# Two decoder layers on one core: first tiles in pieces, whole inverse matrices, inversion levels split around half units

## The reference

```
for l in range(DEPTH):                                   # DEPTH = 2
    h = hybrid_mixer(x, ...)                             # three token mixers in parallel
    x = layer_norm(DN_ALPHA * x + h, ln1_g[l], ln1_b[l])
    f = swiglu(x, ...) if l % 2 == 0 else moe_swiglu(x, router_w, ...)   # 8 experts, top 2
    x = layer_norm(DN_ALPHA * x + f, ln2_g[l], ln2_b[l])

def hybrid_mixer(x, ...):
    proj = x @ w_in                                      # 1024 -> 7936 columns
    o_conv = c_b * short_conv(c_c * c_h, conv_w)         # A: gated convolution
    o_att  = moba_attention(rope(q), rope(k), v)         # B: causal attention, one block of 256
    o_rwkv = rwkv7_time_mix(r, k, v, wl, al, gl, ...)    # C: delta rule with decay
    merged = sum(sigmoid(g_i) * (o_i @ p_i) for the three)
    return merged @ w_out

# the recurrence inside C, per head, for each token t:
S = S * w_t + (S @ -kk_t) (kk_t * a_t) + v_t k_t
y_t = S @ r_t
```

## Time and profile before

| | us |
|---|---|
| median of 3 runs | 1725.62 (1725.05 to 1727.55) |
| the profiled execution's own time | 1726.75 |
| its span, first to last instruction | 1724.8 |
| TensorE matmuls busy | 1686.2 (98% of the span) |
| TensorE's matmuls on the chain that ended last | 89% |
| mean granted clock | 0.990 |

### The profile page before, as it was taken

How to read it: one execution, slowest core, us unless ns; L and a number is a source line. 1 busy time by engine, 2 the same in 40 slices (tenths; PEclk the granted TensorE clock), 3 DMA queues, 4 the chain that set the end, 5 groups by cost and what they waited for, 6 DMA issues and landing times.

```text
span 1724.8 us, 30683 instructions
## 1 busy us (share of the span) xinstructions
PE 1686.2 (98%) x12196; PEld 1496.2 (87%) x12196; DVE 1275.4 (74%) x1223; ACT 1001.0 (58%) x967; POOL 0.9 (0%) x8
## 2 busy tenths in 40 slices
PE   8999999999999999999999999999999999999997
PEld 8899898989999989989988888888888888888886
DVE  5766576474445676567556889898998989898987
ACT  5553463454343645346345777677777677677775
POOL 0000000000000000000000000000000000000000
PEclk9999999999999999999998999999999999999999
DMA  9433332466656353334246999999999999999993
GB/s 288 143 104 99 118 127 77 164 196 189 177 181 207 123 172 99 123 99 131 91 153 220 357 344 392 331 364 353 368 387 324 373 330 392 334 365 338 379 385 139
DMA packets 253186, 411.18 MB, mean 238 GB/s; under 512 B 9376, under 2 KB 134688, under 8 KB 252576
## 3 DMA queue, kind: packets, MB, share of 16 engines
q1 hardware_dynamic: 250832, 400.97, 66.6%
q10 hardware_dynamic: 2256, 8.82, 1.4%
HBM read 407.66 MB, written 2.10 MB: 238 GB/s over the span
## 4 chain that ended last, share of the span: by engine, by line
PE 89%; DVE 5%; ACT 2%; issue 1%; DMA 1%; SPq 0%; ACTq 0%; DVEq 0%
PE W L475 19%; PE W L477 18%; PE W L476 18%; PE Y L475 7%; PE Y L476 6%; PE Y L477 6%; PE Y L707 3%; PE W L612 1%; ACT w_hi L1193 1%; DMA raw<-w_in 1%; DVE w_lo L1668 1%; PE Y L612 1%; DVE sc L1813 1%; PE Y L694 1%; PE Y L771 0%
## 5 line engine op out<-in xcount | busy, mean ns | idle before, releaser
L1668 DVE TENSOR_TENSOR w_lo<-raw,w_hi 128x2048 fp32r<-128x2048 f32 x114 | 261.2, 2292 | 203.5 <-ACT w_hi L1193 202.4
L475 PE MATMUL W<-w_lo,x_hi 128*128 128x512 f32 (+1 forms) x1120 | 389.6, 348 | 1.6 <-DVE x_lo L1978 0.9
L477 PE MATMUL W<-w_hi,x_hi 128*128 128x512 f32 (+1 forms) x1120 | 385.4, 344 | 0.0
L476 PE MATMUL W<-w_hi,x_lo 128*128 128x512 f32 (+1 forms) x1120 | 384.9, 344 | 0.0
L1675 DVE TENSOR_TENSOR w_lo<-raw,w_hi 128x2048 fp32r<-128x2048 f32 x144 | 329.7, 2289 | 45.7 <-ACT w_hi L1199 45.7
L1199 ACT ACTIVATE w_hi<-raw 128x2048 fp32r<-128x2048 f32 x144 | 276.1, 1917 | 72.6 <-PE Y L477 40.0
L475 PE MATMUL W<-x_lo,w_hi 128*128 128x256 f32 x992 | 293.6, 296 | 2.5 <-DVE w_lo L1668 1.1
L1675 DVE TENSOR_TENSOR w_lo<-raw_more,w_hi 128x2048 fp32r<-128x2048 f32 x120 | 275.0, 2291 | 28.2 <-ACT w_hi L1199 27.7
L476 PE MATMUL W<-x_hi,w_lo 128*128 128x256 f32 x992 | 283.4, 286 | 0.0
L477 PE MATMUL W<-x_hi,w_hi 128*128 128x256 f32 x992 | 283.1, 285 | 0.0
L1199 ACT ACTIVATE w_hi<-raw_more 128x2048 fp32r<-128x2048 f32 x120 | 230.5, 1921 | 65.0 <-PE W L477 42.3
(11 more groups left out here) (322 smaller groups left out, 1955.9 us busy)
## 6 DMA issues: line engine op xcount, KB each, us to landing
raw<-w_in SPq DMA_DIRECT2D x124, 512.0 KB, 4.7
raw<-moe_gate SPq DMA_DIRECT2D x48, 1024.0 KB, 6.4
raw<-moe_up SPq DMA_DIRECT2D x48, 1024.0 KB, 7.1
raw<-moe_down SPq DMA_DIRECT2D x48, 1024.0 KB, 5.4
raw_more<-moe_gate SPq DMA_DIRECT2D x40, 1024.0 KB, 7.2
raw_more<-moe_up SPq DMA_DIRECT2D x40, 1024.0 KB, 7.3
raw_more<-moe_down SPq DMA_DIRECT2D x40, 1024.0 KB, 6.4
raw<-w_branch SPq DMA_DIRECT2D x24, 512.0 KB, 4.6
```

Source lines behind the costliest of these rows:

```text
L475: nc.tensor.matmul(out_ap, lhs[0], rhs[1], start=start, stop=False)
L476: nc.tensor.matmul(out_ap, lhs[1], rhs[0], start=False, stop=False)
L477: return nc.tensor.matmul(out_ap, lhs[0], rhs[0], start=False, stop=stop)
L1668: V.tensor_tensor(w_lo[u % 3][:], raw[u % 3][:], w_hi[u % 3][:].bitcast(F32), ALU.subtract)\
```

## The change

**Start.** Units 0, 1 and 2 are loaded and split in pieces (`PIECES`: two quarters and a half for unit 0, halves for units 1 and 2), in turn with x, whose last half is one load. Unit 0's two column halves go to two banks (`W[0]` and `Y[0]`), so that PE can use each piece for both. ACT runs one small copy as soon as its operand is there. Unit 3 is now loaded ahead of `w2` and the constants; 8 warm-up matmuls in place of 11.

**Inversion.** `level` becomes `mx` (first product, its copy on ACT) and `dx` (second product and DVE's additions). In pass 0 `mx` stands between a unit's halves and `dx` behind it; in pass 1 they stay together. `masks` of pass 0 moves ahead of conv unit 2. For `cu` the two column blocks of `xt` are taken as one 128x128 matrix, which needs the lower left quarter cleared: GpSimd (POOL) does so by one memset per pass, and `cu` waits for it.

**Other moves in the table.** `shift 6` moves ahead of rkv unit 0, `rope 3` behind the front of branch0 unit 0, `osplit 2 1` ahead of the back of gate2 unit 3, and DVE makes the low split in the back half instead of the front at qkv unit 3 (`LATE_LOW`). At the three norms whose sums are of split weights, the second token tile's left half is finished first and signalled by `left_sum`. `WARM` loses one matmul at each of two places.

The diff at its core:

```diff
+PIECES = ((0, 0, 2), (0, 2, 4), (0, 4, KD), (1, 0, 4), (1, 4, KD), (2, 0, 4), (2, 4, KD))
+EARLY = [x for x in PIECES if x[2] < KD]
...
-START_WARM = 11
-WARM = {(0, 0): 2, (0, 1): 2, (1, 0): 2, (1, 1): 7, (2, 1): 2}
+START_WARM = 8
+WARM = {(0, 0): 2, (0, 1): 2, (1, 0): 1, (1, 1): 6, (2, 1): 2}
...
-    ("units", "conv", 3, 4), ("level", 0, 1), ("lora_w", 1), ("rate_w", 1), ("shift", 4),
+    ("front", "conv", 3), ("mx", 0, 1), ("back", "conv", 3), ("dx", 0, 1), ("lora_w", 1), ("rate_w", 1), ("shift", 4),
...
+LATE_LOW = (("qkv", 3), ("gate2", 3))
...
-            load_x(0)
-            load_first_half(0, "first_full0")
-            load_x(1)
-            load_first_half(4, "first_full1")
-            load_x(2)
-            load_x(3)
+            for n, piece in enumerate(PIECES):
+                if n < 3:
+                    load_x(n)
+                if n == 5:
+                    sp.dma_start(prm[:], par).then_inc(sem("prm_full"), 16)
+                load_piece(*piece)
...
+                if u == 0:
+                    for a, b in ((0, 2), (2, 4), (4, KD)):
+                        piece_ready(0, a, b)
+                        for m, to in enumerate((bank[:, 0, :], tiles(Y[0][:])[:, 0, :])):
+                            c = slice(m * P, (m + 1) * P)
+                            for k in range(a, b):
+                                if m == 0:
+                                    x_part(0, k)
+                                last = mm3(to, (wh[:, k, c], wl[:, k, c]), (x_hi[:, k, :], x_lo[:, k, :]),
+                                           k == 0, k == KD - 1)
...
+            def last_out(l, u):
+
+                unit_ready(u)
+                wh, wl = (w[u % 3][:].rearrange("p (k c) -> p k c", k=2) for w in (w_hi, w_lo))
+                for h in range(2):
+                    c = slice(h * 512, (h + 1) * 512)
+                    for k in range(2):
+                        last = mm3(Y[2 + h][:], (x_hi[:, 6 + k, P:T], x_lo[:, 6 + k, P:T]), (wh[:, k, c], wl[:, k, c]),
+                                   False, k == 1)
+                    last.then_inc(w_used if h else sem("left_sum"), 1)
...
                 if c == 0:
-                    pe.wait_ge(sem("column_ready"), n + 1)
+                    pe.wait_ge(sem("corner_clear"), n + 1)
                 for h, m, hc, half in HEADS:
-                    nc.tensor.matmul(Y[1][0:HD, hc], xt[0:HD, 4 * c + h, 0, :], g_s[0:HD, h, :], start=True, stop=True)
-                    last = nc.tensor.matmul(Y[1][HD:P, hc], xt[:, 4 * c + h, 1, :], g_s[:, h, :], start=True, stop=True)
+                    whole = xt[:, 4 * c + h].rearrange("p a b -> p (a b)")
+                    last = nc.tensor.matmul(Y[1][:, hc], whole, g_s[:, h, :], start=True, stop=True)
...
-            act.wait_ge(sem("eps_ready"), 1)
+            act.wait_ge(sem("eps_ready"), 3)
+            A(small[:, 52:53], small[:, 9:10], ACT.Copy)
...
+            for n in range(2 * L):
+                if n:
+                    pool.wait_ge(sem("corner_clear"), n)
+                pool.wait_ge(sem("column_ready"), n + 1)
+                pool.wait_ge(sem("dxt_done"), 2 * TOP * (n + 1))
+                nc.gpsimd.memset(xt[HD:P, :, 0, :], 0.0).then_inc(sem("corner_clear"), 1)
...
             def layer_norm(m, t, used):
 
-                if t == 0:
-                    dve.wait_ge(sem("sum_done"), m + 1)
-                else:
-                    dve.wait_ge(w_used, used)
                 for h in range(2):
+                    if t == 0:
+                        dve.wait_ge(sem("sum_done"), m + 1)
+                    elif h == 0:
+                        dve.wait_ge(sem("left_sum"), m + 1)
+                    else:
+                        dve.wait_ge(w_used, used)
```

More of the change, by code:

```diff
@@ L1685, in front @@
                 u = layer_unit(l) + UNIT0[kind] + q
-                if (kind, q) != ("gate2", 3):
+                if (kind, q) not in LATE_LOW:
                     split_lo(u + 2)
@@ L1692, in back @@
                 u = layer_unit(l) + UNIT0[kind] + q
-                if (kind, q) == ("gate2", 3):
+                if (kind, q) in LATE_LOW:
                     split_lo(u + 2)
```

169 lines of the change are left out of this document (96 added, 73 removed), and 3 rows, old and new, of the table TIMELINE.

## The result

| | before | changed kernel |
|---|---|---|
| median, 4 runs each on one chip (us) | 1726.29 (1725.05 to 1727.55) | 1700.54 (1699.06 to 1701.85) |
| ratio | | 0.9851, 95% interval 0.9833 to 0.9868 |
| profiled execution; its span | 1726.75; 1724.8 | 1699.88; 1697.9 |
| mean granted clock | 0.990 | 0.994 |

The change saves 25.75 us by the medians and 26.9 by the profiled executions, where 29.2 were forecast; 1700.54 lies in the range of 1689 to 1704. The sum is close, but its terms are off by up to 2.9 us each, in both directions. To see them I take the same PE instruction in both traces and subtract its start times; I call that PE's lead.

The account below looks back on a forecast made before the run. TensorE (PE), its matmuls filling 98% of the span, bounds the kernel. Terms 3.0 + 9.4 + 1.8 + 1.5 + 10.0 + 1.0 + 2.2 + 0.3 = 29.2 off profiled 1726.75 give 1697.5, median 1696.4 us; 8-in-10 range 1689 to 1704.

Parts of the forecast that it names:

- The start: Unit 0 to `lora_w`: last piece lands at 10.1, unit 1 starts at 15.3, `shift 6` wait goes; -3.0 us, ends 0 and -4.
- the splits at gate2: Early split of `o_lo` under gate2's last half unit removes two PE waits; -2.2 us, ends -1 and -2.4.
- the left sums: Norms: summing the second tile's left half first helps only behind layer 1's mixer; -0.3 us.
- the levels: Inversion levels in two steps: -0.35 us a layer at level 3, -0.55 at the last, others 0; -1.8 in all.
- the clock behind the last level: Behind the inversion's last level: one of two slow-clock stretches goes; -1.5 us, ends 0 and -3.0.
- `cu`: Eight `cu` with whole matrices, eight instructions for 16: 8 x 1.25, -10.0 us; ends 0 and -12.
- the end of pass 0: Scores after pass 0: late low split gives nothing, `rope 3` waits less, -0.5 us a layer; -1.0, ends +1 and -3.
- Rival (a): Gaps at the start and last levels still cool TensorE's clock: 2.5 + 1.5 us less gain, 1700.4; chance 0.20.
- Masks: Masks ahead of the low split: PE's wait before the transpositions and the slow clock go, both layers; -9.4 us, upper end -6.0.
- (b): Rival at `cu`: whole matrices cost what two halves do, 10.0 us less gain, 1706.4; chance 0.08.
- (c): Rival at the inversion levels: ACT becomes their bound, loss 35 us against a gain of 29.2, 1731; chance 0.02.
- (d): Rival: an unseen queue replaces each wait, only `cu` and half of the masks remain, about 1711 us; chance 0.05.

Follow-up runs that it names:

- two_pieces: Changed kernel with unit 0 loaded and split in two halves, not two quarters and a half, and 11 warm-up matmuls, not 8: 1697.94 us, ratio 0.9851.
- warm_gap: Changed kernel with warm-up matmuls added in unit 0's two gaps, one ahead of the second piece and four ahead of the third: 1699.99 us, ratio 0.9848.
- x_first: two_pieces with the last quarter of x split by ACT and DVE ahead of unit 1's first piece, not behind it: 1698.98 us, ratio 0.9842.
- mx_late: Changed kernel with mx and dx of pass 0 together again behind each unit's second half: 1703.82 us, ratio 0.9882.
- cu_halves: Changed kernel with cu as before, the inverse's two column blocks separate, 16 instructions in place of eight: 1710.26 us, ratio 0.9911.
- sums_together: Changed kernel without the left sums: second token tile's halves summed in turn as before, no signal for its left half: 1700.24 us, ratio 0.9853.

## Why the prediction held, and where it did not

**The total: partly luck.** By the terms the forecast is 2.3 us too high. The start (2.9 too high), the splits at gate2 (1.5), the left sums with the norms (0.8) and the levels (0.5) are set off by the clock behind the last level (1.5 too low), `cu` (1.0) and the end of pass 0 (0.9). Rival (a) gave 1700.4, almost the measured 1700.54, and that is luck too: its start came true, but the last levels, for which it counted nothing, gave 3.0 by the clock alone. Two of my own numbers were wrong before any run. The 1688 "for more than I count" takes off the whole ends -3 and -4 where 1 and 2 of them were already in the forecast; added rightly it is 1691.9. And the sign "at the last level about 0.9" doesn't fit the term of 0.55, which leaves 0.64 of 1.19.

**What bounds the kernel.** Right. No term lay off PE, and the expert phase didn't move.

**The start: wrong, 0.1 for 3.0.** The failed step is "the last piece lands at 10.1". I took the bytes ahead of it and one rate; the bytes were right for an order with two halves (9.9 in two_pieces), but with the quarters they came at 11.5 (10.27 to 11.71 in ten traces), and the DMA moved 237 GB/s from 6 to 8 us, where the kernel before had 355. Why the quarters do this stays open. The second failed step is the gap: PE idled 3.0 us, not 1.7, and the clock fell, which warm_gap showed to be 1.5 us. That was rival (a), right in its mechanism at the start. The step that held is `shift 6`: unit 1 started 0.94 later than before, and still `lora_w` came 0.1 earlier, with no wait. A further error would have come next: "3 us of room" for unit 4 was read against PE's need of unit 4 itself, and not against `ss`, which hangs on DVE's and ACT's work behind its splits; x_first lost 3.5 us there, some of it perhaps by that execution's late landing. In the nine traces with this start `lora_w` came at 28.64 to 30.94, 30.1 on average, and the clock fell in all nine, so on average the term is nought and not one execution's bad luck; the best of the nine had 1.3. Of the kernel before there is one trace, 29.98, to set against them.

**Masks: right,** in both layers, the wait and the clock: 9.4 by the two traces, 8.6 when undone, the difference being how long the clock stayed down.

**Levels: right in kind, 0.5 too large.** At level 3 and at the last level PE gained 0.49 a layer each, where I had 0.35 and 0.55. But levels 2, 4 and 5, which I took as nothing, cost 0.1 each, and mx_late got 0.1 back at each. **Clock behind the last level: 1.5 too small.** Both drops went, not one of two. With the old wait of 1.20 one drop of two came back, so the half that I counted was a fair price for chance; what I did not see is that the wait would shrink to 0.52, by more than half.

**`cu`: right in mechanism, 1.0 too small.** I wrote 2.06 less 0.81, 1.25; the eight gained 1.37 each. The traces put the rest ahead of the group: the first half block started 0.21 behind the last projection matmul (148.20 to 148.41 in cu_halves), the first whole matrix 0.12. That a new one takes as long as two old ones, the lower end of the term, is out.

**End of pass 0: 0.9 too small.** That the late split gives nothing was right (0.1 a layer). The 0.84 a layer that is left, where I had 0.5, stands with `rope 3` and what moved with it. It was not undone by itself, so its cause is not shown.

**Splits by need: wrong by 1.5.** The step "ACT's three DMA issues and DVE's low split move behind them, both needed 4 us later" failed. PE needs them later, but ACT's own queue does not wait: issues and a table load now stood ahead of a bank copy, whose low split and merging feed the output units. In layer 0 the whole 1.1 turned into a wait for `w_lo`, which the prediction had named as the sign of its being wrong; in layer 1 0.7 of it is left.

**Left sums: nothing,** forecast 0.3. The 0.44 lost behind layer 0's mixer, which I had at nothing, is not explained; there, kernels whose edits lie elsewhere differ from the changed one by -0.09 to +0.33, so part of it is scatter. **Rivals.** (b) and (c) are out: `cu` went from 2.06 to 0.81, and no level waited longer for ACT. (d), a new queue in the place of the wait, is what happened at the start and at gate2 of layer 0.

## What to carry to other kernels

A saved wait is worth the distance to the next thing that is late, so follow the chain behind it through every engine's queue, not only to the next use by the engine that waited. What an engine issues on the side (DMAs, table loads) is part of its queue: ask what it covered before and what it stands in front of after the move. Price the clock with the waits, as a chance and not as a certainty: waits of 1.2 us dropped it in some layers here and not in others. And compare several executions of a start before putting its delay down to an order of loads.

## What the runs showed of the hardware

- One wait, the same to the hundredth, drops TensorE's clock in one layer and not in the other (1.20 us: 0.72 and 1.00), and with 2.37 us it was at 0.50 and 0.74 in two executions. Waits of 1.34 and 1.83 at `ss` dropped it, 1.67 in unit 0 and 0.90 at `ss` did not.
- With the same loads at the start, the last piece of unit 0 landed 1.4 us apart between executions (10.27 to 11.71 in ten), and in the nine with the same start `lora_w` began up to 2.3 us apart (28.64 to 30.94). No other place differed more between profiled executions with the same instructions.
- A weight load took 130 ns for 64 columns and 192 ns for 128, and the group of sixteen short matmuls with the one 2.05 us, the group of eight with the other 0.81.
- PE can stand still for 0.96 us (mx_late), and at the same inversion for 0.42 us (sums_together), with nothing in the profile to wait for, while other executions with these instructions show no such stop.
